# Three re-orderings in a hybrid decoder step: exponentials of the GDN row factors two places later, the first final norm as 16 items, cross-attention as a pipeline

## The reference, cut to what matters

```
h = rmsnorm(x, norm_w);  proj = h @ w_in
# gated DeltaNet (GDN), 8 heads, 4 chunks of 128 tokens here
decay = exp(where(tril, Gc[i] - Gc[j], -inf))
Amat  = where(strict, (kb @ k.T) * decay, 0);  T = inv(eye + Amat)
attn  = (q @ k.T) * decay;  qg = q * exp(Gc);  k_end = k * exp(g_last - Gc)
u = T @ (v*beta);  wk = T @ (kb*exp(Gc))       # then a scan over the chunks
# cross-attention, 4 heads, 256 memory tokens
s = (q_mem @ mem_k.T) * 128**-0.5;  y_mem = softmax(s) @ mem_v
# the end
out  = (headnorm(y) * mix_norm_w * silu(z)) @ w_out
y    = rmsnorm(x + out, final_norm_w)
```

## Time and profile before

| | |
|---|---|
| three runs, median | 1419.67 us |
| the profiled execution | 1415.74 us, span 1413.9 us |
| PE busy | 1329.5 us (94%) |
| DVE, ACT, POOL busy | 737.9, 650.4, 425.2 us |
| granted TensorE clock, mean | 0.976 |
| chain that ended last | PE 77%, DVE 9%, ACT 7%, issue 4%, POOL 2%, DMA 1% |
| HBM traffic | 144.32 MB read, 15.26 MB written |

### The profile page before, as it was taken

The page is one execution under the profiler, slowest core; times in us unless marked ns, Lnnn a source line. Parts: engine busy times, 40 slices in busy tenths (PEclk is TensorE's granted clock), DMA queues, the critical chain, the costliest instruction groups (busy, mean ns, idle before and its releaser), DMA issues.

```text
span 1413.9 us, 26171 instructions
## 1 busy us (share of the span) xinstructions
PE 1329.5 (94%) x10599; PEld 1289.3 (91%) x10599; DVE 737.9 (52%) x1277; ACT 650.4 (46%) x1291; POOL 425.2 (30%) x426
## 2 busy tenths in 40 slices
PE   7999999899999899999999999999999899998995
PEld 7898989779888899999999999999999899997995
DVE  7845444420566344757575653433433666765553
ACT  7565466422443345454545444534432543354553
POOL 0000010002344345646464645454420212112112
PEclk9999999999999999999999999999999999998998
DMA  7224542153111213232423222222212367755652
GB/s 287 65 98 147 153 164 60 45 175 109 46 56 40 70 47 120 76 107 75 137 76 107 75 78 63 75 61 77 74 60 65 114 233 241 233 200 192 181 186 97
DMA packets 48408, 161.28 MB, mean 114 GB/s; under 512 B 5296, under 2 KB 10832, under 8 KB 48032
## 3 DMA queue, kind: packets, MB, share of 16 engines
q1 hardware_dynamic: 39344, 130.77, 29.5%
q10 hardware_dynamic: 8832, 28.33, 5.8%
q0 software_dynamic: 112, 0.50, 0.1%
HBM read 144.32 MB, written 15.26 MB: 113 GB/s over the span
## 4 chain that ended last, share of the span: by engine, by line
PE 77%; DVE 9%; ACT 7%; issue 4%; POOL 2%; DMA 1%; ACTq 0%; SPq 0%; DVEq 0%; POOLq 0%
PE ps L895 40%; PE ps L1211 15%; PE ps L788 12%; PE ps L852 2%; PE ps L856 2%; PE ps L1179 1%; ACT w_hi L1241 1%; PE ps L1161 1%; POOL w_lo L2124 1%; DVE fin L2112 1%; DVE conv_a L1692 1%; ACT L1398 1%; ACT L1455 1%; DVE conv_a L1811 1%; DVE h_lo L1695 1%
## 5 line engine op out<-in xcount | busy, mean ns | idle before, releaser
L895 PE MATMUL ps<-h_hi,w_hi 128*128 128x260 f32 x1856 | 412.0, 304 | 30.3 <-POOL w_lo L2124 15.0
L1241 ACT ACTIVATE w_hi<-w_raw 128x512 fp32r<-128x512 f32 x424 | 254.7, 625 | 297.2 <-PE ps L895 155.7
L895 PE MATMUL ps<-h_lo,w_hi 128*128 128x260 f32 x1856 | 379.3, 286 | 0.0
L895 PE MATMUL ps<-h_hi,w_lo 128*128 128x260 f32 x1856 | 379.1, 286 | 0.0
L895 PEld LDWEIGHTS ps<-h_hi,w_hi 128*128 128x128 f32 x1856 | 293.9, 194 | 42.3 <-issue 20.3
L2124 POOL TENSOR_TENSOR w_lo<-w_raw,w_hi 128x512 fp32r<-128x512 f32 x156 | 215.8, 1390 | 299.7 <-ACT w_hi L1241 299.7
L895 PEld LDWEIGHTS ps<-h_lo,w_hi 128*128 128x128 f32 x1856 | 292.8, 193 | 0.0
L895 PEld LDWEIGHTS ps<-h_hi,w_lo 128*128 128x128 f32 x1856 | 292.6, 193 | 0.0
L1653 DVE TENSOR_TENSOR w_lo<-w_raw,w_hi 128x512 fp32r<-128x512 f32 x268 | 184.0, 708 | 144.7 <-ACT w_hi L1241 143.1
L1211 PE MATMUL ps<-y_hi,w_hi 128*128 128x260 f32 x640 | 185.3, 289 | 10.1 <-DVE w_lo L1653 4.3
L1211 PE MATMUL ps<-y_lo,w_hi 128*128 128x260 f32 x640 | 183.3, 286 | 0.0
(11 more groups left out here) (373 smaller groups left out, 1970.2 us busy)
## 6 DMA issues: line engine op xcount, KB each, us to landing
w_raw<-in_w_in SPq DMA_DIRECT2D x120, 512.0 KB, 3.6
w_raw<-in_w_out SPq DMA_DIRECT2D x80, 512.0 KB, 3.8
w_raw<-in_w_mem SPq DMA_DIRECT2D x16, 512.0 KB, 3.6
x_t<-in_x_t SPq DMA_DIRECT2D x8, 520.0 KB, 9.5
fin<-in_x_t SPq DMA_DIRECT2D x8, 520.0 KB, 5.9
out_y_t<-fin SPq DMA_DIRECT2D x16, 260.0 KB, 2.3
c_kv<-in_c_k ACTq DMA_DIRECT2D x8, 512.0 KB, 4.4
c_kv<-in_c_v ACTq DMA_DIRECT2D x8, 512.0 KB, 3.6
```

What stands on the lines that cost most here:

```text
L895: last = mm(out[:, hf, :], w, a[:, kk, HALF * hf:HALF * hf + HALF], start=(kk == 0 and j == 0), stop=(kk == KT - 1 and j == 2))
L1241: A(w_hi_of(g)[:, s], raw[:, g % NRAW, s], ACT.Copy).then_inc(sem("w_hi_done"), 1)
```

## The change

Four edits, all of order; no arithmetic is changed.

- Attention becomes a pipeline. The exponential of a cell becomes a step of its own, 3. In round i the list holds scores of cell i, turn and copy of cell i-1, exponential of cell i, values of cell i-2. There is a pause ahead of step 3 as well. PE's turn of cell i now waits for the copy of cell i-1 instead of i-2.
- In each GDN head the five exponentials and DVE's product with q leave step 1 and become the item `gdnexp`, three places behind step 1, two of them pauses; one more pause stands between it and step 2. Steps 2 and later lie one place further back.
- The scaling and the stores of `final 0` become 16 items `fscale` and 8 items `fstore`, one after every third item of what follows, beginning right behind `final 0`. A store stands behind the scaling of a later pair.
- `final 1` scales and stores after its norm as before, in the order of `FIN_ORDER`, which alternates between tiles of DVE and of POOL.

```diff
+FIN_ORDER = (0, 1, 10, 11, 2, 3, 12, 13, 4, 5, 6, 7, 14, 15, 8, 9)
-... "att 1": 1, "decatt0": 3,
+... "att 1": 1, "att 3": 1, "decatt0": 3,
...
-    for h in range(MEM_H):
-        for c in range(NC):
-            att += [("att", h, c, 0), ("att", h, c, 1)]
+    for i in range(MEM_H * NC + 2):
+        if i < MEM_H * NC:
+            att += [("att", i // NC, i % NC, 0)]
+        if 1 <= i <= MEM_H * NC:
+            att += [("att", (i - 1) // NC, (i - 1) % NC, 1)]
+        if i < MEM_H * NC:
+            att += [("att", i // NC, i % NC, 3)]
+        if i >= 2:
+            h, c = divmod(i - 2, NC)
             if c == 0 and h:
                 att += [("atty", h - 1, 1)]
             att += [("att", h, c, 2)]
-        att += [("atty", h, 0)]
+            if c == NC - 1:
+                att += [("atty", h, 0)]
...
+            if s == 1:
+                steps += [("gdn", h, s), PAUSE, PAUSE, ("gdnexp", h), PAUSE]
+                continue
...
+    at_final = outs.index(("final", 0))
+    spaced = []
+    for i, n in enumerate(FIN_ORDER):
+        spaced += [("fscale", 0, n)] if i % 2 == 0 else [("fscale", 0, n), ("fstore", 0, FIN_ORDER[i - 3] if i > 2 else None)]
+    spaced += [("fstore", 0, FIN_ORDER[-2])]
+    rest = outs[at_final + 1:]
+    outs = outs[:at_final + 1]
+    for i, it in enumerate(rest):
+        outs.append(it)
+        if i % 3 == 2 and spaced:
+            outs.append(spaced.pop(0))
...
+    items += [("fscale", 1, n) for n in FIN_ORDER] + [("fstore", 1, n) for n in FIN_ORDER[::2]]
...
-                    if i >= 2:
-                        pe.wait_ge(*upto("a_pt", i - 1))
+                    if i:
+                        pe.wait_ge(*upto("a_pt", i))
```

More of the change, by code:

```diff
@@ L128 @@
 PAUSES = {
-    "ssd 1": 1, "ssdend": 1, "gdn 0": 1, "gdn 1": 2, "gdn 3": 2, "gdn 18": 1, "gdn 22": 1, "gdn 29": 8, "att 1": 1, "decatt0": 3,
+    "ssd 1": 1, "ssdend": 1, "gdn 0": 1, "gdn 1": 2, "gdn 3": 2, "gdn 18": 1, "gdn 22": 1, "gdn 29": 8, "att 1": 1, "att 3": 1, "decatt0": 3,
     "decgdn 0": 1, "decattp": 6, "decatty": 1, "decnorm": 1,
@@ L162 @@
     "gdn_scan_dve": [("g_state", 4), ("g_y_ss", 1), ("g_ms", 1), ("g_y_scaled", 1)],
-    "att_pe": [("a_scores", 1), ("a_turned", 1), ("a_y_ps", 1)],
-    "att_act": [("a_exp", 1), ("a_pt", 1)],
     "att_dve": [("a_max", 1), ("a_nmax", 1)],
@@ L756, in _ @@
                 load_residual((it[1] + 3) // 2)
[L757 to L765, removed]
+            if k == "fstore" and it[2] is not None:
+                cols, n = out_cols(it[1]), it[2]
+                if n < FIN_V:
+                    spe.wait_ge(*upto("scaled_v", FIN_V * it[1] + n + 2))
+                else:
+                    spe.wait_ge(*upto("scaled_g", (KT - FIN_V) * it[1] + n - FIN_V + 2))
+                spe.dma_start(O["y_t"][:, n:n + 2, cols], fin[:, n:n + 2, cols]).then_inc(sem("out_y"), 16)
         spe.wait_ge(*upto("out_mk", 16))
@@ L1103, in _ @@
                     last.then_inc(sem("a_turned"), 1)
-                else:
+                elif s == 2:
                     pe.wait_ge(*upto("a_pt", i + 1))
@@ L1447, in _ @@
                     A(g_s[:, 0, :], g_s[:, 1, :], ACT.Ln, bias=eps[:, 0:1]).then_inc(sem("g_ln"), 1)
[L1448 to L1464, removed]
                 elif 4 <= s < 16 and s % 2 == 1:
@@ L1498, in _ @@
                     A(quad(y_raw[:, h, DB:NT]), quad(side[0]), ACT.Copy).then_inc(sem("g_y_copied"), 1)
+            elif k == "gdnexp":
+                h = it[1]
+                act.wait_ge(*upto("g_rows", h + 1))
+                if h >= 2:
+                    act.wait_ge(*upto("g_y_turned", h - 1))
+                if h == 5:
+                    act.wait_ge(*upto("d_yred", 64))
+                act.wait_ge(*upto("g_sub", 2 * h + 2))
+                A(g_qg(h)[:, :, :], quad(side[3]), ACT.Exp).then_inc(sem("g_qrow"), 1)
+                if h:
+                    act.wait_ge(*upto("g_k_scaled", 2 * h))
+                A(g_s[:, 3, 0:4], g_row[:, 0, :], ACT.Exp).then_inc(sem("g_ea"), 1)
+                act.wait_ge(*upto("g_colt", h + 1))
+                A(g_s[:, 4, 0:4], g_s[:, 4, 0:4], ACT.Exp).then_inc(sem("g_ke"), 1)
+                act.wait_ge(*upto("g_masked", 2 * h + 1))
+                A(g_e1[:, :, :], g_e1[:, :, :], ACT.Exp).then_inc(sem("g_exp"), 1)
+                act.wait_ge(*upto("g_masked", 2 * h + 2))
+                A(g_e2[:, :, :], g_e2[:, :, :], ACT.Exp).then_inc(sem("g_exp"), 1)
             elif k == "att":
@@ L1507, in _ @@
                             cache_load(j)
+                elif s == 3:
                     act.wait_ge(*upto("a_nmax", i + 1))
@@ L1894, in _ @@
                     V.tensor_tensor(g_r1[h % 2][:, :, :], quad(side[1]), along(beta[:, 0:NC, h], P), ALU.mult).then_inc(sem("g_v_scaled"), 1)
-                    dve.wait_ge(*upto("g_qrow", h + 1))
-                    V.tensor_tensor(g_qg(h)[:, :, :], g_qg(h)[:, :, :], quad(gconv[:, 0, DB:NT]), ALU.mult).then_inc(sem("g_qg"), 1)
                 elif s == 2:
@@ L1948, in _ @@
                     V.tensor_tensor(g_qg(h)[:, :, :], quad(side[2]), along(g_s[:, 5, 4:8], P), ALU.mult).then_inc(sem("g_y_scaled"), 1)
+            elif k == "gdnexp":
+                h = it[1]
+                dve.wait_ge(*upto("g_qrow", h + 1))
+                V.tensor_tensor(g_qg(h)[:, :, :], g_qg(h)[:, :, :], quad(gconv[:, 0, DB:NT]), ALU.mult).then_inc(sem("g_qg"), 1)
             elif k == "gdnrow":
@@ L2106, in _ @@
                 V.tensor_tensor(fin[:, n % KT, cols], out_ps(n), fin[:, n % KT, cols], ALU.add).then_inc(sem("fin_added"), 1)
[L2107 to L2112, removed]
+            elif k == "fscale" and it[2] < FIN_V:
+                hb, n, cols = it[1], it[2], out_cols(it[1])
+                if n == 0:
+                    dve.wait_ge(*upto("fin_r", hb + 1))
+                    dve.wait_ge(*upto("fin_weighted", KT * (hb + 1)))
+                V.tensor_tensor(fin[:, n, cols], fin[:, n, cols], fin_r[:, cols], ALU.mult).then_inc(sem("scaled_v"), 1)
     @block.gpsimd
@@ L2238, in _ @@
                     G.tensor_tensor(fin_acc[:, cols], fin_acc[:, cols], fin_sq[:, n % 2, cols], ALU.add).then_inc(sem("fin_acc"), 1)
[L2239 to L2244, removed]
+            elif k == "fscale" and it[2] >= FIN_V:
+                hb, n, cols = it[1], it[2], out_cols(it[1])
+                if n == FIN_V:
+                    pool.wait_ge(*upto("fin_r", hb + 1))
+                    pool.wait_ge(*upto("fin_weighted", KT * (hb + 1)))
+                G.tensor_tensor(fin[:, n, cols], fin[:, n, cols], fin_r[:, cols], ALU.mult).then_inc(sem("scaled_g"), 1)
     ctx.close()
```

## The result

The changed kernel took 1373.41 us (median of four runs, 1372.75 to 1373.91), the kernel before 1418.99 beside it (1415.33 to 1423.92). The ratio is 0.968, 95% interval 0.965 to 0.971. The forecast was 1381 with a range of 1364 to 1402. The profiled execution took 1373.0 us, 42.7 less than the profiled one of before, where the sum of the prediction's terms was 35.9.

A forecast was written before the change was run, and what follows sets the result against it. PE was taken as the bound, busy 1329.5 of 1413.9 us. Terms 15.4 + 8.7 + 10.2 + 1.6 = 35.9 us off the profiled 1415.7 gave 1379.8, put a little above at 1381; range 1364 to 1402.

The forecast's parts named there:

- GDN, 15.4 predicted: GDN heads: PE's seven waits for POOL go, with low-clock stretches; gain 15.4 us, bounds 6 and 23.1.
- heads 1 to 4: GDN heads 1 to 4: each returns between 0 and 2.3 us, taken as 1.0, 4.0 in all; clock 2.5 more.
- `g_p` followed at once: GDN head 1: `g_p` directly follows four state updates of 5.15 us together, so it is ready at 578.9 to 580.8.
- The lock as a price: GDN heads 1 to 4: DVE and GpSimd exclude each other, giving the lower bound, 4.0 us worse than the sum.
- Attention, 8.7 predicted: Attention: waits return 5.5 us and low-clock stretches 3.2, the last turn's 3.3 us wait stays; bounds 3 and 10.9.
- rival 2: GDN heads 1 to 4 return nothing, attention waits at the values instead of the turn; 20.7 us gained, 1395; chance 0.19.
- First norm, 10.2 predicted: Behind the first final norm: PE's waits and low-clock stretches go, 10.7 less 0.5 of slack; bounds 6 and 10.7.
- The very end, 1.6 predicted: Last stores: alternating order puts POOL's pairs between, two transfers fewer left when DVE ends; gain 1.6 us, bounds 0 and 1.6.
- everything returns: Rival: GDN, attention, norm and end all reach their upper bounds, 46.3 us gained, 1369; chance 0.17.
- The waits change place: The same as rival 2: GDN heads 1 to 4 and attention return nothing, 1395; chance 0.19.
- Stores hold up loads: Rival, first final norm: a store in SP's list delays the next loads and eats the 10.2 us, 1390; chance 0.08.
- The ladder: Rival, GDN heads 1 to 7: each of twelve ladder steps loses one product, 61 us in all, 1456; chance 0.04.

The follow-up runs named there:

- GDN alone: The kernel before with only the move of the GDN exponentials: 1397.82 us, ratio 0.987 (0.984 to 0.989).
- attention alone: The kernel before with only the attention pipeline: 1409.71 us, ratio 0.994 (0.992 to 0.996).
- norm and end alone: The kernel before with only the spread first final norm and the other order at the end: 1409.21 us, ratio 0.992 (0.989 to 0.996).

## Why the prediction was right, point by point

**GDN, 15.4 predicted, 20.2 measured.** The mechanism for the seven waits is the predicted one, shown by putting the exponentials back. Heads 5 to 7 returned their waits whole, but for 0.40 in head 7. The term that was too small is heads 1 to 4. There the step "`g_p` followed at once" kept its order but not its time: the four updates took 4.09 instead of the 5.15 that was assumed, and `g_p` was ready when PE came. The wait came one step earlier, at `g_t`, which the prediction's own bounds had as late as 575.0 in the numbers of before. PE's step there:

```profile
576.19 0.56 PE L788 MATMUL ps<-g_t,g_natm 128*128 128x128 f32 x4
```

Without the 2.3 us it starts at 573.9, and 575.0 is 1.1 later: the measured wait. The sum looked at `g_p` alone. So the four heads returned 1.2 each (2.3 less 1.1), where 1.0 was taken; of its bounds of 0 and 2.3 the upper one was too high by its own times, which give 1.8 (580.7 less 578.9). The larger miss is the clock: half of the stretches of heads 1 to 4 were to stay, 2.5 us; all went, and no wait of 1.1 us in any kernel brought one. And head 0, set at a few tenths, lost its waits of 0.70 and 1.16 but for 0.19.

**The lock as a price.** By the exclusive lock of the Trainium skill ("SBUF — State Buffer", section "SBUF: two separate sides") the prediction had heads 1 to 4 come out 4.0 us worse. `g_tt` without POOL's split agrees with the rule (0.68 us against 1.77), and the gate moved by two steps fits that the order of meetings decides (8.8 us in GDN). But it did not bring the lower bound: before, head 1's four updates took 0.78, 1.37, 1.25 and 1.98 us, all of them drawn out, in the changed order three were, and with the gate moved four again. The prediction did not work out which it would be.

**Attention, 8.7 predicted, 9.0 measured, partly for other reasons.** The turns' waits went whole and the last turn's stayed, as forecast. But the waits fell only by 4.6 (length less busy went from 13.5 to 8.9), not 5.5: values that wait for the copy of the head before, and a split behind DVE's chain, were not in the sum, and the clock returned 1.6 of a predicted 3.2. Beside that PE was busy 2.8 us less on the same matmuls. Of that the values are a part; before and after (count, busy us, mean ns, idle ahead):

```profile
L1109 PE MATMUL ps<-mv,att_pt 128*128 128x128 f32 x64 | 11.4, 304 | 2.6 <-ACT att_pt L1517 1.3 <-ACT y_raw L1527 1.2
```

```profile
L1128 PE MATMUL ps<-mv,att_pt 128*128 128x128 f32 x64 | 9.9, 276 | 2.5 <-ACT y_raw L1548 2.5
```

The second half of rival 2 (waits at the values) was thus there in small, 2.5 us.

**First norm, 10.2 predicted, 10.9 measured** (12.5 of the last stretch less 1.6 of the end): both waits and both stretches went, and the slack of 0.5 was not used up. **The very end, 1.6 predicted, 1.6 measured.** No run tests the order at the end without the spread of the first norm. SSD's 1.5 us was in no term: one stretch of half clock there was absent. That is chance: GDN alone, with the order of before up to there, took 144.07 us too.

**The rivals.** By time alone the measured 1373.4 is nearer to "everything returns" (1369) than to the forecast (1381), and 0.4 inside the end of the 1373 to 1390 that got the forecast's chance. What speaks against that rival are the waits that stay, 1.1 us in each of heads 1 to 4 and 3.5 at the last turn; it named the right end for GDN's clock. "The waits change place" failed: GDN alone gained 1.3%. "Stores hold up loads" failed: SP's loads go between the stores and PE doesn't wait. The ladder did not lose a product: from step 2 of a head on PE stands over 0.35 us nowhere but at `g_t`, once in a head at most.

**Where the 6.8 us between sum and measurement come from:** GDN 4.8, SSD 1.5, the norm 0.7, attention 0.3, less 0.3 and 0.2 at the start and in the first part of the output. The clock returned 2.8 more than the terms in GDN and 1.5 in SSD, but 1.6 less in attention, where 2.8 of shorter matmuls made up for it. That the sum comes so near is in part luck: in executions with the same order attention took 256.80 and 259.36 us, GDN 598.99 and 605.08, and the clock terms were priced on one trace.

## What to carry to other kernels

An engine that stands for another in the middle of an item holds back everything queued behind it: look in the row of the waiting engine for work that needs nothing from the wait, and put it ahead; that, not more distance, returned 18 of GDN's 20 us. When a wait is removed by more distance alone, look what else queues behind the same chain, since it will be the next to be late. Where VectorE and GpSimd both work from SBUF, put what the critical engine needs ahead of the other work on VectorE, because each of its instructions with both operands in SBUF may wait out one of GpSimd's.

## What the runs showed of the hardware

- PE's waits of 1.9 to 2.3 us for POOL were followed by a stretch at half clock in 21 of 28 cases, at 1.7 us each as a rule, and which ones differs between executions of the same order. The spreads fit that, though no run tested it: the kernel before ranges over 8.6 us, attention alone over 7.2 and norm and end alone over 11.1; the changed kernel and GDN alone, without these waits, over 1.2 and 2.4.
- On DVE a scaling of 128x260 took 0.43 us where it began just ahead of POOL's, and 0.97 where POOL was already at one; the ten at the end took 6.71, 0.67 each, beside six of POOL.
- Instructions of DVE that read PSUM (`g_t`, `g_p`, the scalings of k) took 0.68 to 0.69 us beside the same work of POOL. Of the 128x512 instructions of a GDN head in the changed kernel only those with both operands in SBUF grew: the gate to 1.21, `g_tt` to 1.78.
